# Sixteen columns of padding in the rows of the split weights of a two-layer decoder step

## What is computed

```python
def conv_ffn(u, buf, w_up, conv_w, conv_b, w_down):       # u: rows x 2048
    g, a = jnp.split(u @ w_up, 2, axis=-1)                # w_up: 2048 x 11008
    ext = jnp.concatenate([buf.astype(g.dtype), g], axis=1)
    gc = conv_b + sum(conv_w[j] * ext[:, j:j + S] for j in range(CONV_WIDTH))
    return (jax.nn.silu(gc) * a) @ w_down, ext[:, -CONV_PAD:]

proj = u @ w_in                                           # w_in: 2048 x 6152, the mixer of layer 0
q, k, v, o, gates = jnp.split(proj, [...], axis=-1)
...
return h.astype(u.dtype) @ w_out, state                   # w_out: 2048 x 2048
```

## Time and profile before

| | us |
|---|---|
| median of three runs | 2729.91 (2729.54 to 2730.79) |
| span of the profiled execution | 2730.8 |
| PE busy | 2631.1 (96%) |
| PEld busy | 2523.8 (92%) |
| DVE busy | 1405.0 (51%) |
| ACT busy | 1004.8 (37%) |
| POOL busy | 222.7 (8%) |
| DMA | 389.77 MB, mean 143 GB/s |

### The profile page before, as it was taken

How to read it: one execution, slowest core, us unless ns; L and a number is a source line. 1 busy time by engine, 2 the same in 40 slices (tenths; PEclk the granted TensorE clock), 3 DMA queues, 4 the chain that set the end, 5 groups by cost and what they waited for, 6 DMA issues and landing times. The chain is left out here.

```text
span 2730.8 us, 44822 instructions
## 1 busy us (share of the span) xinstructions
PE 2631.1 (96%) x16761; PEld 2523.8 (92%) x16761; DVE 1405.0 (51%) x2094; ACT 1004.8 (37%) x1345; POOL 222.7 (8%) x306
## 2 busy tenths in 40 slices
PE   7999999999999999999999997599999999999998
PEld 5969789797999999999999997599999999999997
DVE  5444444444754454454445446965455454554545
ACT  4323333233443332333333336244343342333435
POOL 1110201102200000000000003610000000000002
PEclk9999999999999999999999998799999999999999
DMA  4545445454344444444444434144444444444443
GB/s 137 163 153 164 164 124 166 156 163 162 125 143 149 144 140 141 140 140 133 151 144 133 147 128 134 48 142 149 153 144 151 149 147 149 146 149 148 141 141 108
DMA packets 224748, 389.77 MB, mean 143 GB/s; under 512 B 25829, under 2 KB 53045, under 8 KB 223965
## 3 DMA queue, kind: packets, MB, share of 16 engines
q1 hardware_dynamic: 222511, 382.93, 44.0%
q10 hardware_dynamic: 2045, 4.00, 0.4%
HBM read 363.40 MB, written 23.43 MB: 142 GB/s over the span
## 5 line engine op out<-in xcount | busy, mean ns | idle before, releaser
L1019 DVE TENSOR_TENSOR w_lo<-w_raw,w_hi 128x1024 fp32r<-128x1024 f32 x664 | 815.9, 1235 | 1043.8 <-ACT w_hi L759 1041.5
L759 ACT ACTIVATE w_hi<-w_raw 128x1024 fp32r<-128x1024 f32 x664 | 699.0, 1058 | 1364.6 <-PE bank L419 1328.8
L417 PE MATMUL bank<-xh,w_hi 128*128 128x336 f32 (+2 forms) x3584 | 1135.6, 317 | 49.6 <-issue 23.2
L418 PE MATMUL bank<-xl,w_hi 128*128 128x336 f32 (+2 forms) x3584 | 1129.7, 315 | 0.0
L419 PE MATMUL bank<-xh,w_lo 128*128 128x336 f32 (+2 forms) x3584 | 1127.4, 315 | 0.0
L417 PEld LDWEIGHTS bank<-xh,w_hi 128*128 128x128 f32 x3584 | 676.7, 189 | 58.5 <-issue 44.9
L419 PEld LDWEIGHTS bank<-xh,w_lo 128*128 128x128 f32 x3584 | 678.5, 189 | 0.0
L418 PEld LDWEIGHTS bank<-xl,w_hi 128*128 128x128 f32 x3584 | 677.7, 189 | 0.3
L417 PE MATMUL bank<-hh,w_hi 128*128 128x336 f32 (+1 forms) x1632 | 511.7, 314 | 4.5 <-issue 4.5
L419 PE MATMUL bank<-hh,w_lo 128*128 128x336 f32 (+1 forms) x1632 | 511.4, 313 | 0.0
L418 PE MATMUL bank<-hl,w_hi 128*128 128x336 f32 (+1 forms) x1632 | 511.3, 313 | 0.0
(11 more groups left out here) (247 smaller groups left out, 1257.4 us busy)
## 6 DMA issues: line engine op xcount, KB each, us to landing
w_raw<-in_w_up SPq DMA_DIRECT2D x640, 256.0 KB, 2.8
w_raw<-in_w_down SPq DMA_DIRECT2D x336, 256.0 KB, 3.4
w_raw<-in_w_mlstm_in SPq DMA_DIRECT2D x192, 256.0 KB, 3.1
area<-in_state_mlstm_C SPq DMA_DIRECT2D x32, 512.0 KB, 5.3
w_raw<-in_w_mlstm_out SPq DMA_DIRECT2D x64, 256.0 KB, 3.0
out_C_sample<-area SPq DMA_DIRECT2D x32, 512.0 KB, 3.0
w_raw<-in_w_up SPq DMA_DIRECT2D x64, 192.0 KB, 2.5
w_raw<-in_w_pool SPq DMA_DIRECT2D x16, 256.0 KB, 3.1
```

The lines of the kernel that those rows point to most:

```text
L417: pe.matmul(out, wh, xhk, start=first, stop=False)
L418: pe.matmul(out, wh, xlk, start=False, stop=False)
L759: nc.scalar.activation(w_hi[:, s], w_raw[:, s], ACT.Copy).then_inc(hi_done, 1)
L1019: V.tensor_tensor(w_lo[:, s], w_raw[:, s], w_hi[:, s].bitcast(F32), ALU.subtract).then_inc(lo_done, 1)
```

## The change

Rows of `w_hi` and `w_lo` become 528 columns (2112 bytes) long, of which the first 512 are used. `w_raw` stays as it is. Row 2s + j of a weight tensor now begins 64 x (2s + j) bytes further, modulo 256, than row 0. The two tensors grow by 512 bytes a partition each. Room for them comes from small tiles that now share one allocation: `gh` and `negeye` in `small`, `hcol` and `warm` in `cols`, `eps` in the last column of `rc` (whose 1/16 is no longer written), `bg` in `area`, which shrinks by 20 columns.

```diff
@@ -36,6 +36,7 @@
 CW = 512
+WROW = CW + 16
 SLOTS = 4
@@ -113,8 +114,9 @@
         w_raw = sb("w_raw", [P, SLOTS, 2, CW])
-        w_hi = sb("w_hi", [P, SLOTS, 2, CW], F32R)
-        w_lo = sb("w_lo", [P, SLOTS, 2, CW], F32R)
+        w_hi_rows = sb("w_hi", [P, SLOTS, 2, WROW], F32R)
+        w_lo_rows = sb("w_lo", [P, SLOTS, 2, WROW], F32R)
+        w_hi, w_lo = w_hi_rows[:, :, :, 0:CW], w_lo_rows[:, :, :, 0:CW]
@@ -127,25 +129,24 @@
-        eps = sb("eps", [P, 1])
-        warm = sb("warm", [P, 1])
...
-        negeye = sb("negeye", [H, H])
+        small = sb("small", [P, 8])
+        gh, negeye = small[:, 0:4], small[0:H, 4:4 + H]
...
-        hcol = sb("hcol", [P, 3, 2])
+        cols = sb("cols", [P, 8])
+        hcol, warm = cols[:, 0:6].rearrange("p (s a) -> p s a", a=2), cols[:, 6:7]
...
-        gh = sb("gh", [P, 4])
-        bg = sb("bg", [36, 1])
         rc = sb("rc", [P, 16])
+        eps = rc[:, 15:16]
...
-        AREA = 15700
+        AREA = 15680
@@ -185,6 +186,7 @@
+        bg = view(15616, 1, 36)
@@ -1357,7 +1359,7 @@
-            for t in range(16):
+            for t in range(15):
                 G.memset(rc[:, t:t + 1], 1.0 / (t + 1))
```

## The result

| | before | changed |
|---|---|---|
| median of seven runs, us | 2730.28 (2729.54 to 2732.76) | 2738.94 (2736.91 to 2740.19) |
| ratio | 1 | 1.003 (95% interval 1.002 to 1.0039) |
| span of the profiled execution, us | 2730.8 | 2738.4 |

A forecast was written before the change was run, and what follows sets the result against it. TensorE's closely following matmuls were taken to bound the kernel. Terms of -8.9 (c0 = 0), +1.1 (c0 = 14) and 0 for the rest gave -7.8 us against 2729.9, hence 2722 us, range 2712 to 2732.

The forecast's parts named there:

- What bounds the kernel, and that alignment matters: TensorE's matmul spacing sets the time; chunks alternate between 3.675 and 3.72 us with the input's offset, perhaps its distance from the weights.
- two weak signs: Weight loads begin with a matmul, and loads reach 192 ns beside inputs at 128 and 192; both favoured the distance.
- The rival in which the input's own offset decides: Inputs at 128 and 192 stay slow wherever the weights lie: 2729.9 us, plus or minus 1; chance 0.30.
- Products with c0 = 0: Matmuls of 336 columns: 197 slow chunks of 394 each gain 45 ns, 8.9 us less; bounds 5.9 and 17.8.
- a further gain above it: If distance 0 beats 64 by the same step again, all 394 chunks with c0 = 0 gain another 8.9 us.
- The third load: Beside each third matmul the chunk's other row is loaded, 64 off; giving its third of the gain back leaves 5.9 us.
- The long loads as a sign: Loads of up to 192 ns, against 187 to 188, in the chunk with inputs at 128 and 192: the streams meet.
- c0 = 14 and c0 = 16: Later products, 322 and 320 columns: 1.1 us more for c0 = 14; 0 for c0 = 16, bounds 0.7 us either way.
- ScalarE, VectorE, GpSimd, DMAs and small tiles: Writes with a gap, one memset fewer, shifted views: all taken as 0, hidden under the matmuls or off the path.
- The rival on the other side: Weights off offset 0 are slower, or equal starts meet most; all chunks go to the slow level: 2739.9 us, chance 0.12.

The follow-up runs named there:

- the shift by 32 columns: The kernel before, without padding, with `w_hi` and `w_lo` moved by 32 columns (128 bytes) against the inputs: ratio 0.9999.
- the rows outermost: Each chunk runs row j = 0 for all four output tiles, then j = 1: ratio 1.002 on the kernel before, 1.0003 on the changed kernel.
- the padding by slot: The changed kernel with 32 columns behind each slot of two rows in place of 16 behind each row: 2720.76 us, ratio 0.996.
- the shift by 32: The changed kernel, rows padded, with all weight rows moved on by 32 columns (128 bytes): 2743.4 us, ratio 1.0041 against before.
- a spacer: The kernel before, unpadded, with weights moved by 32 columns, by 16, or `w_lo` alone by 16: ratios 0.9999, 1.0032 and 1.0014.

## Why the prediction was wrong

**What bounds the kernel, and that alignment matters: right.** TensorE's pace is the time, and the position of the weights against the input changes it, by up to 1.7% of a chunk (3.656 to 3.72 us). The weights had never moved in the trace of before, so it rested on two weak signs; the shift by 32 columns shows it. The rival in which the input's own offset decides is refuted. The Trainium skill ("TensorE: Matmul & The Clock Gate", Part 2, the step on LDWEIGHTS) says that loading the next weights takes no read bandwidth from the running matmul. What the prediction drew from it, that the distance can't matter, does not hold in this kernel: 3.67 and 3.72 us change places when only the weights move. Whether that is read bandwidth or something else, no run here shows.

**Products with c0 = 0, the term that failed.** It read "taking the whole better chunk as the level that all reach", 8.9 us less; measured are 7.1 us more. The better chunk holds distances 0 and 64 in turn, with all three loads of a tile alike. The changed kernel has 0 and 0, and a third load that is 64 off. I took the equal offset to be the cause of the good level, with 64 as its dilution, and even counted a further gain above it. The runs show no such thing. With the rows outermost, distance 0 alone gives 3.696 and 64 alone 3.684; both are slower than the two in turn, 3.656. The layout that really repeats the better chunk, the padding by slot, gains more than the term said. The step also took for granted that a layout has one level. The changed kernel ran ten chunks at 3.656 and 256 at 3.716 with the same offsets. Why it falls into the slow level nearly always stays open.

**The third load.** The step saw it, and let it give back "its third of the gain" at most. The rows of before have no tile with unlike loads, so nothing there bounded its cost from above; it should have had a bound beyond zero gain. That a third load matters is shown by the run with `w_lo` alone moved, 10 ns a chunk. How much of the changed kernel's level is its doing isn't shown.

**The long loads as a sign.** From loads of 192 ns in the slow chunk I read that short loads mean little contention. Those rows are of the loads of `w_lo` alone; in the same fast chunk of before one load of `w_hi` took 191 ns. The duration of a load does not tell the pace. The changed kernel with the rows outermost has all 192 loads of eight chunks at 187 or 188 ns, at 3.696 us a chunk, and the padding by slot has the same loads at 3.656.

**c0 = 14 and c0 = 16: right.** 0.9 us more where 1.1 was forecast, and 0.7 less, at the edge of the bounds of 0.7.

**ScalarE, VectorE, GpSimd, DMAs and small tiles: right, all 0** within what can be measured, by the rows above and by the run with the small tiles alone.

**The rival on the other side** had the time, 2739.9 against 2738.9, with a chance of 0.12, but not the mechanism. That the load "meets it most just when both begin alike" is not what the runs show: distance 0 alone is middling, and 192 is the slowest with the rows outermost. Its other half, rows off offset 0, is refuted by the shifts: with all weight rows of before moved to offset 128 the time stays. So the agreement of its number is luck. Its objection, that distance 0 is in the fastest chunk, was the same misreading as the forecast's. The range ended at 2732 because I left this rival out of it.

What the chip does when the reads meet isn't settled. Levels depend on pairs, a fast chunk behind a slow one starts slow, and one product runs at 3.703 us a chunk in one pass and at 3.724 in the next (the shift by 32). All this speaks for a state that outlives a matmul and is set when a product starts; no run here shows what it is.

## What to carry to other kernels

A fast stretch is evidence for the whole arrangement in it, not for the one feature that looks like its reason: before a layout is built on a level read from a trace, list all that is alike in that stretch (here the pair 0 and 64, and three like loads), and copy the list. Read a level from several stretches before you take it for the layout's own. Where matmuls follow back to back as here, with 4-byte operands and a load for each, the layout of the weights against the input may be worth a try; other kernels were not measured. Here, in the kernel's own order of matmuls, a spacer moved the time by 0 to 0.3% upward, padding by row by 0.1 to 0.4% upward, and padding by slot by 0.4% downward. With the rows outermost, padding by row left the time of before as it was, and took 0.25% off it when the weights were also moved by 48 columns. Aligned addresses are not a goal in themselves.

## What the runs showed of the hardware

- The pace of back-to-back matmuls with 4-byte operands depends on where the weights that are loaded meanwhile lie against the moving operand. Moving the weights alone by 128 bytes made 3.67 and 3.72 us change places. Over the layouts tried, the same 24 matmuls ran from 3.656 to 3.73 us with 336 columns, and from 3.496 to 3.544 in the stretches with 320.
- One layout can have several levels. Chunks with the same instructions, slots and offsets took 3.656 or 3.716 us in the changed kernel, and 3.696 and 3.711 in turn or 3.724 with the shift by 32. A level holds through a product.
- With the rows outermost at 336 columns, the moving operand 64 bytes ahead of the weights is the best distance, 0 the second, 128 the third and 192 the worst (1.83, 1.85, 1.86, 1.87 us for 12 matmuls). Padded rows at 320 columns give the same order by the first two loads (3.496, 3.510, 3.523, 3.544 us for 24). With the rows outermost at 320 columns the four are within 3 ns. Mixed pairs don't follow from these by adding.
- The duration of a weight load does not show the pace: loads of 187 and 188 ns throughout at 3.656 and at 3.696 us a chunk.
- Writing 1024 elements as two runs of 512 with a gap costs neither ScalarE (1060 and 1059 ns) nor VectorE (1225 and 1226 ns).
